# Products that nobody reads in TensorE's waits: behind four turns of table E and during the copies of the kernel table

## The reference, cut to what matters

```python
xr = jnp.einsum('ntgc,gpc->ntgp', ug, bbr)          # 64 groups of 16 channels, 64 states each
xi = jnp.einsum('ntgc,gpc->ntgp', ug, bbi)
_, _, hr, hi = lax.associative_scan(combine, (a_r, a_i, xr, xi), axis=1)
y = (jnp.einsum('ntgp,gcp->ntgc', hr, c_re) - jnp.einsum('ntgp,gcp->ntgc', hi, c_im))
y = jax.nn.gelu(y.reshape(n, t, D_MODEL) + d_skip * uf)
z = y @ w_glu
```

## Time and profile before

| what | value |
|---|---|
| median of 3 runs | 2788.67 us (2784.19 to 2790.56) |
| profiled execution | 2787.05 us |
| its span | 2785.1 us |
| mean granted TensorE clock | 0.978 |
| TensorE busy | 2663.0 us (96%) |
| VectorE busy | 1365.6 us (49%) |

### The profile page before, as it was taken

The page is one execution under the profiler, slowest core; times in us unless marked ns, Lnnn a source line. Parts: engine busy times, 40 slices in busy tenths (PEclk is TensorE's granted clock), DMA queues, the critical chain, the costliest instruction groups (busy, mean ns, idle before and its releaser), DMA issues.

```text
span 2785.1 us, 44457 instructions
## 1 busy us (share of the span) xinstructions
PE 2663.0 (96%) x18614; PEld 2541.8 (91%) x18614; DVE 1365.6 (49%) x2259; ACT 841.7 (30%) x1699; POOL 264.9 (10%) x433
## 2 busy tenths in 40 slices
PE   5589999999999999999999999989999999999998
PEld 4489999999999999988888888857999999999998
DVE  7982235423332333866666767676354333233325
ACT  6231122211221122335455454564131112111212
POOL 2200000000000000012142422430000000000000
PEclk7789999999999999999999999999999999999999
DMA  3512111111111111322335545386111111111101
GB/s 99 82 37 60 46 33 54 38 46 54 45 37 45 55 46 35 107 78 72 80 80 130 123 116 134 86 325 257 46 46 46 46 45 45 45 45 45 45 31 63
DMA packets 174430, 205.13 MB, mean 74 GB/s; under 512 B 47334, under 2 KB 129622, under 8 KB 174024
## 3 DMA queue, kind: packets, MB, share of 16 engines
q1 hardware_dynamic: 149040, 156.63, 18.7%
q0 software_dynamic: 19776, 43.87, 5.8%
q10 hardware_dynamic: 5472, 2.66, 0.6%
HBM read 156.73 MB, written 27.69 MB: 66 GB/s over the span
## 4 chain that ended last, share of the span: by engine, by line
PE 80%; DVE 6%; issue 2%; ACT 2%; POOL 1%; DMA 1%; DVEq 0%; ACTq 0%
PE PS L221 12%; PE PS L218 12%; PE PS L217 12%; PE PS L403 9%; PE PS L400 9%; PE PS L399 9%; PE PS L2290 4%; PE PS L2291 3%; PE PS L2292 3%; PE PS L2321 2%; PE PS L2348 2%; PE PS L2335 1%; DVE SSB L2214 1%; DMA CB<-C_SCRATCH 1%; DVE SQ L191 1%
## 5 line engine op out<-in xcount | busy, mean ns | idle before, releaser
L217 PE MATMUL PS<-XH,WH 128*128 128x352 f32 x1920 | 617.3, 322 | 4.0 <-PEq L103 3.8
L218 PE MATMUL PS<-XL,WH 128*128 128x352 f32 x1920 | 618.9, 323 | 0.0
L400 PE MATMUL PS<-HIDL,WH 128*128 128x352 f32 x1536 | 494.5, 323 | 0.0
L399 PE MATMUL PS<-HIDH,WH 128*128 128x352 f32 x1536 | 493.3, 322 | 0.0
L221 PE MATMUL PS<-XH,WL 128*128 128x352 f32 x1920 | 414.9, 324 | 0.0
L217 PEld LDWEIGHTS PS<-XH,WH 128*128 128x128 f32 x1920 | 362.2, 189 | 4.6 <-issue 4.5
L218 PEld LDWEIGHTS PS<-XL,WH 128*128 128x128 f32 x1920 | 361.0, 188 | 0.1
L350 DVE TENSOR_TENSOR H<-PS,H 128x1056 f32<-128x1056 f32 x128 | 160.8, 1256 | 400.3 <-PE PS L403 400.1
L403 PE MATMUL PS<-HIDH,WL 128*128 128x352 f32 x1536 | 331.6, 324 | 0.0
L221 PEld LDWEIGHTS PS<-XH,WL 128*128 128x128 f32 x1920 | 329.4, 188 | 0.0
L330 DVE TENSOR_TENSOR TMP<-TMP 128x1056 f32<-128x1056 f32 x64 | 80.6, 1259 | 472.6 <-ACT TMP L293 472.4
(11 more groups left out here) (399 smaller groups left out, 3401.7 us busy)
## 6 DMA issues: line engine op xcount, KB each, us to landing
RAW<-w_up SPq DMA_DIRECT2D x32, 1024.0 KB, 5.4
RAW<-w_down SPq DMA_DIRECT2D x32, 1024.0 KB, 4.9
KVR<-cache_kv_w SPq DMA_DIRECT2D x18, 1024.0 KB, 11.2
QB<-QA SPq DMA_DIRECT2D x120, 132.0 KB, 2.6
ARAW<-w_q SPq DMA_DIRECT2D x24, 512.0 KB, 4.6
O_SCRATCH<-OT POOLq DMA_DIRECT2D x96, 128.0 KB, 3.0
OB<-O_SCRATCH POOLq DMA_DIRECT2D x24, 512.0 KB, 7.5
RAW<-w_glu SPq DMA_DIRECT2D x16, 512.0 KB, 4.8
```

The lines of the kernel that those rows point to most:

```text
L217: nc.tensor.matmul(out, wh(k), xh[:, k, c], start=(k == 0), stop=False)
L218: nc.tensor.matmul(out, wh(k), xl[:, k, c], start=False, stop=False)
L399: nc.tensor.matmul(out, w, m.hidh[:, k, q], start=(k == 0), stop=False)
L400: nc.tensor.matmul(out, w, m.hidl[:, k, q], start=False, stop=False)
```

## The change

A function `spin(n, bank)` multiplies the identity with itself n times, as 128x128 fp32 products into columns 384 to 511 of one PSUM bank. Nobody reads the result, no semaphore counts it and it waits for none. TensorE runs 14 such products behind each of `turn_e(0..3)`, 100 between units 3 and 4 of `turn_x`, and 16 behind unit 8, ahead of the wait for `k_out`: 172 in all. Nothing else is changed.

```diff
@@ -1248,8 +1248,14 @@
+        def spin(n, bank):
+
+            for i in range(n):
+                nc.tensor.matmul(ps[:, bank, 384:512], m.ident[:], m.ident[:], start=(i == 0), stop=(i == n - 1))
+
         for ch in range(4):
             turn_e(ch)
+            spin(14, 5)
         for ch in range(4):
             for b in range(4 * ch, 4 * ch + 4):
                 turn_u(b)
@@ -1310,8 +1316,12 @@
-        for u in range(UNITS // 2):
+        for u in range(4):
             turn_x(u)
+        spin(100, 7)
+        for u in range(4, UNITS // 2):
+            turn_x(u)
+        spin(16, 7)
         pe.wait_ge(f.k_out, 1024)
         pe.wait_ge(f.h_kept, UNITS // 2)
         pe.wait_ge(f.k_kept, 4)
```

## The result

The changed kernel takes 2791.32 us in the median of 12 runs (2787.57 to 2793.12), the kernel before 2786.54 us in 12 runs around them. The ratio is 1.0016, with a 95% interval of 1.0009 to 1.0023: between 2.5 and 6.4 us slower. The profiled execution took 2793.12 us, with a span of 2791.3 us against 2785.1.

What follows compares the result with a forecast made beforehand. TensorE, busy 2663.0 of 2785.1 us, was taken to bound the kernel. +0.5 at table E and +3.4 at the copies gave +3.9 on 2787.05, 2790.95 us; forecast median 2792, own range 2788 to 2794.6, 8 in 10 2785 to 2798.

Steps and rivals of the forecast that it cites:

- What bounds the stage: State stage: TensorE's chain is later from 126 to 156 us, so lateness counts in full; VectorE's slack 3.02 us.
- the same work behind the same waits: Rest of TensorE's chain behind the copies: unchanged apart from shifts in the clock, ±1.5 us.
- The price of a product: One added product: 0.225 us at full clock, 0.43 at half; 100 products take 22.5 us.
- Term A: Turns of table E, four runs of 14: mostly covered by waits or repaid; +0.5 us, range −2 to +3.
- Term B: Copies of the kernel table, runs of 100 and 16: 5.4 us late, 2.0 back; +3.4 us, bounds +1.3 to +6.5.
- The sum and the range: Whole kernel: +3.9 us on the profiled execution, given as 2792 us; own range 2788 to 2794.6.
- The first: Rival for both places: waits are well filled, a gain, 2785.2 us; chance 0.15.
- The second: Rival: turns behind every run fall back to half clock, repayments fail; +7.2 us, 2794.3; chance 0.06.
- The third: Rival: products and samples' load both late behind busy DMA engines; +8 to +10 us, 2795 to 2797; chance 0.20.

Runs made afterwards that it cites:

- e1: Only the four runs of 14 products behind the turns of table E, added to the kernel before; 2787.28 us against 2786.37, ratio 1.0002.
- e4: Changed kernel without runs at table E, with 88 products between units 3 and 4, 20 ahead of unit 8, none behind it; 2787.01 us.
- e9: e8 plus 14 products behind each of the first three turns of table E; ratio 0.9972 to the kernel before.
- e8: Kernel before, with the tiny sample transposes and ScalarE's copies of them moved behind the last turn of table E; 2779.98 us, ratio 0.9974.
- e7: e4 with 80 instead of 88 products between units 3 and 4 and 16 instead of 20 ahead of unit 8; 2783.64 us, ratio 0.9993.
- e10: e9 plus 80 products between units 3 and 4 and 16 ahead of unit 8; 2779.29 us, ratio 0.9965.

## Why the prediction was right, point by point

- **What bounds the stage.** Right for 50 to 156 us: the 3.7 us by which TensorE's x units were late went into VectorE's wait (6.40 us; about 6 was forecast), and its operation behind the wait started 3.3 us later. For the part behind it, where I took "the same work behind the same waits" on TensorE's chain, it was VectorE's chain that carried: from C to the gate product it is 63.4 to 64.4 us in all twelve kernels of the table, however fast TensorE was. After, TensorE regained 3 us by 177 us and waited 1.22 us for VectorE at 191.75, where it was 1.9 us behind the kernel before. The clock fell behind that wait (0.50 in 195 to 197 us), the next eight turns took 1.80 and not 1.09 us, and the stage ended 2.75 us later, not 3.9. So "the same work behind the same waits" was the weak step of the sum, within the ±1.5 us that it was given.
- **The price of a product.** 100 took 22.50 us, exactly the 22.5 of the sum; a run of 14 took 3.29 us at full clock (3.15).
- **Term A, +0.5.** It was +0.3, with the clock held through the 1.52 us ahead of the second turn. Measured from the first turn `turn_u` started 2.0 us late and not 2.4, since the runs of 3.29 us with turns of 1.06 just fitted into the waits. That the clock falls again in the tiny transposes was right. The kernel e1 confirms the term against this one profile, and in the time only to within 0.1%, which is ten times the term; that three profiles without the runs reached W earlier leaves its mean open.
- **Term B, +3.4.** It was 3.65 us at the x units. The load was taken to land at 134.8 (134.70), the 16 products at 5.5 us (5.62), the start of the products with `T` at 140.8 (140.81), their new length at 1.8 us (1.99). Two misses cancelled in the load: it was issued 1.3 us later and not 2.2, and took 5.9 us where 5.2 were in effect assumed. The sum was thus closer to the measured 0.4 us at unit 8 than its parts. The run of 16 alone costs as much, without it nothing is left, with 32 it costs 4.0 us more.
- **The sum and the range.** 2792 against 2791.32; 4.8 us by the medians against 3.9 by the sum, which the interval (2.5 to 6.4 us) holds. That the absolute time fits within 1 us is partly luck: 2792 was added up on a median before of 2788.67 us, and the one measured beside the changed kernel was 2786.54. The forecast's own range mixes bases too, with its lower end counted from 2787.05 us and its upper from about 2789; from 2788.67 alone, +1 to +5.6 us is 2789.7 to 2794.3. The profiled execution had 6.2 us more span, of which 3.5 lie behind the state stage. That "rest" was 2563.3 to 2568.6 us over the twelve profiles, without a pattern: 2564.3 with the 16 products alone and 2568.6 in a kernel whose time was the same as before. I take it for the position at which the clock happens to fall in the samples' stages, but nothing here forces that position, so this stays argued. The state stage explains 2.75 us of the 4.8, and the profiles don't say where the other 2 us of the medians are.
- **The rivals.** The first (well filled waits) fails at the 16 products, as was said; with the runs around the copies covered (e4) the gate product came 1.0 us nearer to W, and the time was the same. The second, that transposes let the clock fall, is refuted for those of 128x128 (in the tiny ones it did fall): the turns behind the runs took 1.07, 1.06 and 1.91 us. Clearer still is e9, where TensorE did nothing but transposes from 48.03 us to the increments: the granted clock was 1.00 from 48 to 64 us, and the last 16 transposes of `turn_u`, at 57.93, took 1.91 us. The Trainium skill (TensorE: Matmul & The Clock Gate, Part 4: PE-mode transpose) says otherwise, and the measurement decides. The third (a late load or fetch) did not come: there was no stall in the run of 100, and the load took 5.9 us. ScalarE's issues did take 1.0 us longer, but behind a run that was itself 1.8 us too long this cost nothing.

## What to carry to other kernels

Filling a wait with useless products is worth what the next work gains by the full clock, and only if the filling ends ahead of the wait's release and the gain reaches the engine that binds: here the 16 products ahead of ready work took 5.6 us and brought back 1.7 at the products behind them, the second 16 brought back nothing, and the covered runs brought the state stage 1.0 us (e4) to 1.9 us (e9 against e8), neither of which shows in the time. Before filling, look for what makes the clock fall or the chain long and isn't needed yet: moving 65 tiny transposes off the chain gave 6.5 us by the medians (0.16 to 0.36%), without any filler.

## What was not expected of the hardware

- With nothing changed ahead of it, VectorE's start on table W differed by 2.6 us from one execution to another (66.65 and 69.27), by the moment at which TensorE's clock rose and fell. A single profile is no measure for a change of this size.
- A gap of 1.52 us between the first run and the turn behind it left the clock full. The clock of the kernel with 1.63 us ahead of unit 8 (e7) fell to half, that of the one with 0.83 us (e4) stayed, but in e10 it stayed full through 2.13 us ahead of the second turn, which took 1.07 us. The length of the gap alone doesn't decide.
- 128 records of the products with `T` took 3.64 us at half clock and 1.99 at full, so they follow the clock down to 16 ns a record. In one kernel out of the five with them at full clock TensorE stood still for 1.18 us right behind.
